# Chunk-wise modulation, a folded bias, a running sum for the mean, and alternating heads in a float32 transformer kernel

## What is computed

```python
def mixer_layer(x, cx, c, c_ctx, w_in, w_out, w_ada, b_ada, ln_g, ln_b, ...):
    alpha = (2.0 * DEPTH) ** 0.25
    shift, scale, gate = jnp.split(jax.nn.silu(c) @ w_ada + b_ada, 3, axis=-1)
    h = x * (1.0 + scale[:, None]) + shift[:, None]          # modulation
    ... = jnp.split(h @ w_in, SPLIT_AT, axis=-1)
    y_a, yc_a = hgrn2_mixer(...)                             # the scans
    ...                                                      # three attentions: y_b, y_c, y_d
    y = jnp.concatenate([y_a, y_b, y_c, y_d], axis=-1) * jax.nn.silu(g_lat)
    x_new = layer_norm(alpha * x + gate[:, None] * (y @ w_out), ln_g, ln_b)

def layer_norm(x, g, b):
    mu = jnp.mean(xf, axis=-1, keepdims=True)
    var = jnp.mean(jnp.square(xf - mu), axis=-1, keepdims=True)
    return (xf - mu) * lax.rsqrt(var + LN_EPS) * g + b

def step(s, xs):                                             # gla_chunk_scan, per head
    bcum = jnp.cumsum(fc, axis=1)
    o_inter = jnp.einsum('bthk,bhkv->bthv', qf * jnp.exp(bcum), s)
    att = jnp.einsum('bthk,bshk,btshk->bhts', qf, kf, decay)
    o_intra = jnp.einsum('bhts,bshv->bthv', att, vf)
    s_new = jnp.exp(blast)[..., None] * s + jnp.einsum('bshk,bshv->bhkv', kf * jnp.exp(blast - bcum), vf)
```

## Time and profile before

| | us |
|---|---|
| median of three executions | 3739.03 |
| lowest and highest | 3736.16, 3740.89 |
| the profiled execution | 3741.47 |
| its span | 3739.7 |

### The profile page before, as it was taken

One profiled execution on the slowest core, in us unless ns is written; L12 is line 12 of the kernel. 1 busy time (PEld: TensorE's weight loads), 2 busy tenths in 40 slices (PEclk: granted clock), 3 DMA queues, 4 the chain that ended last, 5 costly groups with the idle time before them and its releaser, 6 DMA issues. The chain is left out here.

```text
span 3739.7 us, 53123 instructions
## 1 busy us (share of the span) xinstructions
PE 3302.9 (88%) x20584; PEld 2477.3 (66%) x20584; DVE 1722.9 (46%) x2662; ACT 1125.0 (30%) x1939; POOL 1213.7 (32%) x998
## 2 busy tenths in 40 slices
PE   7999889999999989998999887879898867788787
PEld 5888668777777767776787675546565555456454
DVE  4344754335533464444343665444543365445433
ACT  3222332213322231113222233334343234434332
POOL 3444434444344432222444442203211132213211
PEclk9999999999999999998999998789899988789889
DMA  3222212333233311111333310000001110000011
GB/s 130 96 96 96 79 68 107 127 133 109 92 133 118 117 69 57 57 57 57 118 113 135 118 40 18 18 18 30 18 18 68 40 54 26 23 22 26 23 51 40
DMA packets 73774, 263.03 MB, mean 70 GB/s; under 512 B 7792, under 2 KB 9072, under 8 KB 73200
## 3 DMA queue, kind: packets, MB, share of 16 engines
q1 hardware_dynamic: 67104, 242.25, 17.9%
q10 hardware_dynamic: 6480, 18.11, 1.3%
HBM read 250.89 MB, written 7.34 MB: 69 GB/s over the span
## 5 line engine op out<-in xcount | busy, mean ns | idle before, releaser
L850 POOL TENSOR_TENSOR wl<-raw,wh 128x1024 fp32r<-128x1024 f32 x320 | 792.2, 2476 | 1216.6 <-ACT wh L959 705.3
L1301 PE MATMUL ps<-xh,wh 128*128 128x512 f32 x2400 | 919.2, 408 | 106.4 <-POOL xl L887 37.2
L1301 PE MATMUL ps<-xl,wh 128*128 128x512 f32 x2400 | 867.1, 386 | 0.0
L1301 PE MATMUL ps<-xh,wl 128*128 128x512 f32 x2400 | 864.5, 385 | 0.0
L1301 PEld LDWEIGHTS ps<-xh,wh 128*128 128x128 f32 x2400 | 446.5, 197 | 286.9 <-issue 173.3
L838 POOL TENSOR_TENSOR wl<-raw,wh 128x1024 fp32r<-128x1024 f32 x90 | 219.1, 2435 | 971.7 <-ACT wh L937 971.7
L959 ACT ACTIVATE wh<-raw 128x1024 fp32r<-128x1024 f32 x224 | 237.6, 1061 | 982.5 <-PE ps L1301 929.2
L1301 PEld LDWEIGHTS ps<-xl,wh 128*128 128x128 f32 x2400 | 444.6, 197 | 94.9 <-issue 13.9
L1301 PEld LDWEIGHTS ps<-xh,wl 128*128 128x128 f32 x2400 | 442.1, 195 | 88.3
L1301 PE MATMUL ps<-ah,wh 128*128 128x512 f32 x1104 | 437.4, 403 | 24.8 <-issue 13.5
L1301 PE MATMUL ps<-al,wh 128*128 128x512 f32 x1104 | 420.5, 388 | 0.0
(11 more groups left out here) (337 smaller groups left out, 3726.6 us busy)
## 6 DMA issues: line engine op xcount, KB each, us to landing
raw<-wts_dram SPq DMA_DIRECT2D x458, 512.0 KB, 3.4
spilled_dram<-hc ACTq DMA_DIRECT2D x1, 3072.0 KB, 8.7
hc<-spilled_dram ACTq DMA_DIRECT2D x1, 3072.0 KB, 11.6
hc<-x_dram ACTq DMA_DIRECT2D x8, 256.0 KB, 9.3
spilled_dram<-hc ACTq DMA_DIRECT2D x1, 2048.0 KB, 7.2
hc<-spilled_dram ACTq DMA_DIRECT2D x1, 2048.0 KB, 9.2
out_dram<-hc SPq DMA_DIRECT2D x8, 256.0 KB, 2.0
hc<-ctx_dram ACTq DMA_DIRECT2D x1, 1024.0 KB, 12.1
```

What stands on the lines that cost most here:

```text
L850: pool.tensor_tensor(wl[:, n % SPLIT, :], raw[:, LOADED[n] % RAW, :], wh[:, n % SPLIT, :].bitcast(F32), ALU.subtract).then_inc(lo_done, 1)
L1301: ins = pe.matmul(out_, w[:, s, k * P:(k + 1) * P], x_(k, at), start=first, stop=last)
```

## The change

Seven edits in one:

1. `products` and `advance`: near and far products alternate between the two heads. The two products of the carried state (`qi` by `state`) take only the 64 partitions of their head, and the update of the state is two products of 64 x 64 in place of one of 128 x 128.
2. `mix`: DVE adds chunks 0 to 6 up in `h_sum`, and PE multiplies by ones twice, for `h_sum` and for chunk 7, in place of eight times.
3. The norm's bias: in layer 0 the second DVE instruction of the loop is gone. The bias is folded into the shift of layer 1 (`ada_terms`) and into the step that scales `hc` by alpha in layer 1. In layer 1 ACT adds it.
4. Modulation is a DVE step within the loop that makes the chunk (`modulated`, in `add_f` and in `mix`). ACT computes `xh` straight from `hc` with scale and bias, and stores `hc` to DRAM afterwards. The slots lie elsewhere in `work`.
5. In the last feed-forward part the root goes to `rs` in SBUF, and in all three parts with sums for ada DVE takes them before `add_f`.
6. The gate bounds and lambdas are computed in the first feed-forward part.
7. `first_two_tiles` of a mixer layer runs tile 1 three chunks behind tile 0 (`lag=3`).

```diff
-            def high_parts(parts):
-                for src, hi, lo in parts:
-                    act.wait_ge(part_ready, c.take("part") + 1)
-                    act.activation(hi, src, ACT.Copy).then_inc(part_hi, 1)
...
             def ada_phase(layer):
-                act.wait_ge(h_ready, c.at("h") + KC)
+                base = c.at("h")
                 act.wait_ge(cond_in, 48)
+                for k in range(KC):
+                    act.wait_ge(h_ready, base + k + 1)
+                    for s, (at, w) in enumerate(((0, SEQ), (SEQ, CTX))):
+                        ins = act.activation(xh[:, k, at:at + w], hc[:, k, at:at + w], ACT.Identity,
+                                             bias=ada[:, layer, k, s:s + 1], scale=ada[:, layer, KC + k, s:s + 1])
+                    ins.then_inc(part_hi, 1)
                 act.dma_start(spill[:, :, 0:out_tiles(layer) * P], hc[:, :, 0:out_tiles(layer) * P]).then_inc(h_stored, 16)
-                high_parts(x_parts(layer))
...
-                    for h in range(2):
-                        r = slice(HEAD * h, HEAD * (h + 1))
-                        for l in range(NLOW):
-                            for b in range(P // BLK):
-                                g = slice(t * P + b * BLK, t * P + (b + 1) * BLK)
+                    for l in range(NLOW):
+                        for b in range(P // BLK):
+                            g = slice(t * P + b * BLK, t * P + (b + 1) * BLK)
+                            for h in range(2):
+                                r = slice(HEAD * h, HEAD * (h + 1))
...
                     for h in range(2):
+                        r = slice(HEAD * h, HEAD * (h + 1))
+                        pe.matmul(out_banks[:, h, :], qi[s % 2][r, :], state[r, h * HEAD:(h + 1) * HEAD], start=True, stop=False, skip_group_check=True)
+                    for h in range(2):
                         vv = sv[:, t * P + h * HEAD:t * P + (h + 1) * HEAD]
-                        oo = out_banks[:, h, :]
-                        pe.matmul(oo, qi[s % 2], state[:, h * HEAD:(h + 1) * HEAD], start=True, stop=False, skip_group_check=True)
-                        pe.matmul(oo, far[:, h, :], vv, start=False, stop=False, skip_group_check=True)
+                        pe.matmul(out_banks[:, h, :], far[:, h, :], vv, start=False, stop=False, skip_group_check=True)
...
-                pe.matmul(state_bank, kdt, sv[:, t * P:(t + 1) * P], start=True, stop=True).then_inc(step_full, 1)
+                for h in range(2):
+                    one = slice(HEAD * h, HEAD * (h + 1))
+                    ins = pe.matmul(state_bank[one, one], kdt[:, one], sv[:, t * P + h * HEAD:t * P + (h + 1) * HEAD], start=True, stop=True)
+                ins.then_inc(step_full, 1)
...
-                    first_two_tiles(ways_)
+                    first_two_tiles(ways_, lag=3)
...
-                    if m:
-                        add_mean(m - 1)
-                give(add_mean(KC - 1), p2d, "p2d")
+                add_mean(h_sum, False)
+                give(add_mean(hc[:, KC - 1, :], True), p2d, "p2d")
...
+            def modulated(layer, k):
+
+                x0 = c.at("x")
+                if k == 0:
+                    dve.wait_ge(cond_in, 48)
+                if k >= 2:
+                    dve.wait_ge(x_ready, x0 + k - 1)
+                for s, (at, w) in enumerate(((0, SEQ), (SEQ, CTX))):
+                    ins = dve.tensor_scalar(x_slot(k)[:, at:at + w], hc[:, k, at:at + w], ada[:, layer, KC + k, s:s + 1], ada[:, layer, k, s:s + 1], ALU.mult, ALU.add)
+                ins.then_inc(part_ready, 1)
...
+            def ada_terms():
+
+                own(dve.tensor_scalar(ada[:, :, KC:2 * KC, :], ada[:, :, KC:2 * KC, :], 1.0, None, ALU.add))
+                for s in range(2):
+                    shift, b = ada[:, 1, 0:KC, s], lt[:, 0:KC]
+                    own(dve.tensor_tensor(b, col("lnb", 0, KC), ada[:, 1, KC:2 * KC, s], ALU.mult))
+                    own(dve.tensor_tensor(shift, shift, b, ALU.add))
+                own(dve.tensor_scalar(col("lnb", 0, KC), col("lnb", 0, KC), ALPHA, None, ALU.mult))
...
+                    if m in range(1, KC - 1):
+                        own(dve.tensor_tensor(h_sum[:, 0:n], hc[:, 0, 0:n] if m == 1 else h_sum[:, 0:n], hc[:, m, 0:n], ALU.add))
+                    if m >= KC - 2:
+                        signal(d2p, "d2p")
...
-                    own(dve.scalar_tensor_tensor(hv, hv, col("lng", layer * KC + k), banks(6, n), ALU.mult, ALU.mult))
-                    give(dve.tensor_scalar(hc[:, k, 0:n], hc[:, k, 0:n], col("lnb", layer * KC + k), None, ALU.add), h_ready, "h")
+                    if layer == DEPTH - 1:
+                        c.take("d2a")
+                        dve.scalar_tensor_tensor(hv, hv, col("lng", layer * KC + k), banks(6, n), ALU.mult, ALU.mult).then_inc(d2a, 1)
+                    else:
+                        give(dve.scalar_tensor_tensor(hv, hv, col("lng", layer * KC + k), banks(6, n), ALU.mult, ALU.mult), h_ready, "h")
+                        modulated(layer + 1, k)
```

More of the change, by code:

```diff
@@ L897, in _ @@
                 if name == "pool":
+                    c.take("part ready", KC)
                     for what, m in POOL_TILES:
@@ L1009, in ffn @@
                 h_parts("ffn", layer, i)
+                if (layer, i) == (0, 0):
+                    get(d2a, "d2a")
+                    nsp(lt[:, 8:12])
+                    get(d2a, "d2a")
+                    give(act.activation(lt[:, 16:16 + 2 * DEPTH], lt[:, 16:16 + 2 * DEPTH], ACT.Exp), a2d, "a2d")
                 if (layer, i) == (1, 0):
@@ L1268, in mix @@
                 give(act.activation(b, b, ACT.Exp, scale=-0.5), a2d, "a2d")
-                c.take("h", KC)
+                if layer == DEPTH - 1:
+                    for k in range(KC):
+                        get(d2a, "d2a")
+                        act.activation(hc[:, k, 0:SEQ], hc[:, k, 0:SEQ], ACT.Identity, bias=col("lnb", layer * KC + k)).then_inc(h_ready, 1)
+                else:
+                    c.take("h", KC)
             for dst, src in ((cn[:], con), (pr[:], par), (area(0, NMASK), masks), (area(NMASK, NLEV), levels)):
@@ L1948, in x_low, with add_f @@
                 dve.scalar_tensor_tensor(xl[:, k, 0:SEQ], hc[:, k, 0:SEQ], gain(k), xh[:, k, 0:SEQ].bitcast(F32), ALU.mult, ALU.subtract).then_inc(x_ready, 1)
-            def add_f(gain, *after):
+            def add_f(gain, name, *at):
                 r = rstd()
+                if name == "ada":
+                    r = rs
                 for k in range(KC):
@@ L2534, in _ @@
             c.take("h", KC)
-            run = dict(ffn=ffn_phase, pool=pool, keep=lambda: None, dilated=dilated, ada=ada_phase, mixers=mixers, mix=mix)
+            run = dict(ffn=ffn_phase, pool=pool, keep=lambda: None, dilated=dilated, ada=lambda layer: None, mixers=mixers, mix=mix)
             for name, *rest in PHASES:
```

125 lines of the change are left out of this document (59 added, 66 removed).

## The result

| | before | changed |
|---|---|---|
| median of four executions, us | 3739.96 | 3688.36 |
| lowest and highest | 3736.16, 3743.59 | 3683.62, 3696.72 |
| the profiled execution | 3741.47 | 3696.72 |
| its span | 3739.7 | 3694.9 |

The ratio of the times is 0.9866, with a 95% interval of 0.9849 to 0.9883. The forecast from the median was 3690.6 us; the time is 3688.4. In a later measurement the same kernel gave 3688.05 us (3679.84 to 3695.59) and a ratio of 0.9863 [0.9848, 0.9878]. The profiled execution of the changed kernel was the slowest of its four. So I also show the profile of that second measurement (`after_again`, the same program), whose span was 3678.1 us.

The account below looks back on a forecast made before the run. PE paces the scans, a DVE, ACT, POOL chain the hand-overs. Terms -25 + 4.6 + 0 + 0.3 - 5.8 - 4.4 - 14.7 - 3.4 = -48.4 from median 3739.0 give 3690.6 us, range 3677 to 3704.

Parts of the forecast that it names:

- Scans: 40 scan steps, heads alternating in near, far and advance: 0.96 us a step, 38 us of PE work, minus 25 kept.
- rival A: Scan products keep their pace, bound by something other than array rows; 5 of 25 us stay, 3711; chance 0.16.
- The advance: Carried-state products in each scan step, split into 64-row halves by head: net 0.3 us saved, bounds loss 0.1, gain 0.5.
- Rival B: Scan products overlap, but two thirds of PE's saving goes into longer waits; 25 becomes 9, 3707; chance 0.12.
- Rival C: Near products halve too and shorter products start DVE's chain earlier; 25 becomes 42, 3674; chance 0.11.
- Ada sums: Feed-forward blocks: DVE takes PE's turned sums before add_f, PE idles; two blocks lose 2.05 + 0.2 each, plus 4.6 us.
- Hand-over to layer 0: Last feed-forward block to mixer layer 0: all DVE work excludes POOL, period 4.0 us; zero, bounds minus 4, plus 6.
- The ring: In hand-overs PE has nothing else to do; a chain DVE, ACT, POOL sets the time, microsecond for microsecond.
- Output mix: Mean's sums moved from PE to DVE, which becomes the bound: minus 5.8 us in layer 0, minus 4.4 in layer 1.
- Norm and modulation: Norm and hand-over into layer 1, one interleaved loop with period 2.65 us: minus 14.7, bounds minus 10 and minus 17.
- Rival E: DVE and POOL exclude each other, interleaving hides nothing in layer 1: 5 us less gained, 3697; counted within forecast's 0.54.
- The end: Final loop: eight DVE steps of 0.78 us, ACT adding the bias one chunk behind; minus 3.4 us, bounds minus 2, minus 4.

Follow-up runs that it names:

- near in series: Changed kernel with near products ordered so successive passes use the same column group and row half: near 2.45 us a step instead of 0.95, layer 1 19.5 us longer.
- late sums: Changed kernel with DVE taking the ada sums behind the add_f loop, in the last part behind its first chunk: 3674.38 us, again 3677.52.

## Why the prediction was right

The time came out 2.3 us below the forecast. The sum was right for partly wrong reasons in its largest term, and with some luck. Outside the scans the two pairs of profiles give -21.1 and -25.1 us where -23.4 was forecast. The scans, scaled from layer 1, give 18.5 us where 25 was forecast. That makes 40 to 44 us, and the median fell by 51.6. The 8 to 12 us between lie, as far as the profiles show, in layer 0, and no experiment puts them down to an edit.

1. **Scans.** The forecast had three parts. Far: 0.45 us forecast, 0.46 measured, right. Near: 0.72 forecast, 0.95 measured, no gain at 2.4 GHz. I had taken the middle between no gain and half, and the end of no gain was the truth. The earlier trace rows held the number that spoke for it, 10 ns a pass for 32 columns that alone take 13 ns at 2.4 GHz, and rival A named it. A was right for near and wrong for far. The advance: 0.3 us a step forecast (in it, a guess of 0.1 us for one more change of the array's shape, which no row showed), 0.06 measured in the median step and 0.26 in the mean over all steps, and no time seen in layer 1. PE saved 27.6 us over all steps, not 38: 0.8 in near, 16.4 in far, 5.8 in the products of qi and far with v, 0.7 in the lows and 3.9 in the state product. The share that is kept was too low in its turn: I took two thirds, while in layer 1 the whole of far arrives and near in series shows 81%. The two misses offset each other in part. Scaled from layer 1 (7.4 us for 16 steps) the term is 18.5 us; the two pairs of profiles give 23.5 and 36.5, the excess lying in layer 0 and its clock. Rival B, that the time lands in waits, holds for the advance only. Rival C has the total of the second pair, but not its mechanism: near did not halve.
2. **Ada sums.** The wait is as forecast, 2.4 us in the part without a slow turn; 1.7 to 1.8 us of it arrive in each of the two parts in the second profile. Not foreseen: on the path, the turn is exposed to a fall of the clock. It took 5.1 to 5.4 us in one of the three places in 10 of the 13 profiles behind the change, and cost 1.8 us where DVE waited.
3. **Hand-over to layer 0.** Forecast 0, measured -0.7. The period was 3.77 us, not 4.0, because two of the three DVE instructions run beside ACT's 1.31 us (forecast 1.1) and only the addition meets POOL. The ring named in the first section is the right picture; "all DVE work excludes POOL" was close in number only. The gates' 0.3 us can't be told: in the 13 profiles behind the change the first turn starts between 0.5 us earlier and 1.7 us later than before.
4. **Output mix.** 2.17 and 1.51 us a chunk, forecast 2.2 and 1.5; -5.2 and -4.1 against -5.8 and -4.4. DVE's sum was blocked once for 2.82 us by a POOL remainder, as allowed for.
5. **Norm and modulation.** -14.7, as forecast, with a period of 2.58 against 2.65. The experiments put 4.9 of it to the interleaving, which the forecast's text made the main cause. Rival E, an interleaving that hides nothing, holds in front of layer 0 and not in front of layer 1. (Its price didn't add up: a period of 3.6 us is 6.6 us less gained, not 5, and only so comes to 3697.) The lag, which the forecast counted on to take PE's wait and its time at the lower clock away, gives 1.2 us here.
6. **The end.** ACT's last bias ends 4.3 us earlier, the span 4.1, where 3.4 was forecast. ACT's eight additions keep pace one chunk behind:

```profile
3686.16 5.36 DVE L2545 SCALAR_TENSOR_TENSOR hc<-hc,pr,ps 128x512 f32<-128x512 f32 x8 [5.75 <-ACT ps L1271]
...
3686.95 5.33 ACT L1275 ACTIVATE hc<-hc,pr 128x512 f32<-128x512 f32 x8 [0.90 <-DVE hc L2545]
```

DVE needs 0.67 us a chunk in a row, not 0.78. Instructions that don't wait for each other overlap at their ends.

## What to carry to other kernels

Before you let products take turns over parts of the array, divide the time of the group by its passes and compare that with the columns of a pass: far, at 72 ns for 64 columns, had something to give, near, at 10 ns for 32, had not. When you move a wait ahead of a loop, ask what the awaited work would cost at half clock, and put it behind the first thing that doesn't need it. When stages repeat within 0.3 us and one doesn't, judge an edit by the stages that repeat.

## What was unexpected in the hardware

**The pace of small products.** Passes in one place of the array start 31 to 32 ns apart. Passes that change place start 5 ns apart for the first 32 and, after a stop of 0.08 us, 8.3 ns apart, whatever the columns (16 or 32). So here a better order gained in the first 32 passes and nothing over 96.

**A long run of small matmuls starves PE.** 96 passes in a row never stopped; 192 in a row stopped in 22 places for 0.3 to 2.7 us, each time until 1.2 to 1.6 us after the next packet of instructions had landed.

**The same program, at two clocks.** The two profiles of the changed kernel, the same work in the middle of layer 0. First, then second:

```profile
2400.00:2530.00 130.00, 99.36 (x759) 67.13 (x760) 54.61 (x109) 43.47 (x116) 12.84 (x18) 0.82 0.05 17
```

```profile
2390.20:2512.40 122.20, 91.86 (x760) 63.07 (x761) 54.53 (x109) 43.15 (x116) 12.55 (x16) 0.89 0.06 18
```

Over the whole layer 13.1 us lie between a mean of 0.89 and one of 0.92. I read this as small shifts deciding, where PE waits often, whether the clock falls, and a fall delaying what comes next; that order of cause and effect was not shown.

**A coin toss between DVE and POOL.** In layer 0 a conversion on DVE and a remainder on POOL start 0.14 to 0.15 us apart in every profile. The changed kernel (DVE, POOL), then the one with late sums:

```profile
2202.70 5.00 DVE L2427 CAST ah<-work 128x256 fp32r<-128x256 f32 x1 [0.15 <-DVE work L2423]
...
2202.84 2.40 POOL L839 TENSOR_TENSOR wl<-raw,wh 128x1024 fp32r<-128x1024 f32 x1
```

```profile
2192.48 0.34 DVE L2441 CAST ah<-work 128x256 fp32r<-128x256 f32 x1
...
2192.63 2.45 POOL L839 TENSOR_TENSOR wl<-raw,wh 128x1024 fp32r<-128x1024 f32 x1
```

In 5 of 14 profiles, that of before among them, the conversion took 4.7 to 5.0 us, in 9 it took 0.33. It is not only the remainder that held it: POOL's short instructions behind that followed without a gap, and the conversion ended 2.5 us after the remainder had. The page "SBUF — State Buffer" of the Trainium skill, section "Who interferes with whom", has the two engines share one pair of ports as an exclusive lock; the lost tosses agree, but last over many POOL instructions. In the won ones, too, one of POOL's short instructions was running when the conversion started (in the last rows above one from 2192.38 to 2192.68 us), and it did not hold it.
